# Two heads decoded at a time, peer_v rows summed four at a time, and four moved steps in a hybrid decoder step

## The reference

```python
u, q, k, v, qi, ki, wi, g_conv, g_attn = project_inputs(x, pos, w_in)     # one big projection, rotary, GLU
conv_out = conformer_conv(u, prev, ...)                                    # 31 taps per channel, norm, silu, projection
attn_out = attention over the keys that the indexer's top-k selects        # prompt: 128 of up to 512; sample: 256 of 1028
m = sigmoid(g_conv) * conv_out + sigmoid(g_attn) * attn_out
h = layer_norm(ALPHA * x + m @ w_out, ln1)

def peer_ffn(h):
    q1, q2 = halves of h @ peer_w_query                                    # 8 heads, 2 x 64
    t1, i1 = top_k(q1 @ peer_keys1, 16)                                    # of 128 keys
    t2, i2 = top_k(q2 @ peer_keys2, 16)
    ts, j = top_k(t1[:, None] + t2[None, :], 16)                           # of 256 candidates
    eidx = (i1 * 128 + i2) at j                                            # 16 experts of 16384 a head
    g = softmax(ts)
    a = gelu(h . peer_u[eidx])                                             # 128 rows of 1024 a token
    return sum over (g * a) * peer_v[eidx]                                 # 128 rows of 1024 a token

y = layer_norm(ALPHA * h + peer_ffn(h), ln2)
```

## Time and profile before

| what | us |
|---|---|
| median of 3 runs | 2096.13 |
| lowest, highest of them | 2087.34, 2105.51 |
| the profiled execution's own time | 2089.12 |
| its span, first to last instruction | 2087.3 |
| DVE busy | 1282.2 (61%) |
| PE busy | 1449.6 (69%) |
| POOL busy | 1205.3 (58%) |
| moved by DMA | 682.74 MB, 327 GB/s in the mean |

### The profile page before, as it was taken

How to read it: one execution, slowest core, us unless ns; L and a number is a source line. 1 busy time by engine, 2 the same in 40 slices (tenths; PEclk the granted TensorE clock), 3 DMA queues, 4 the chain that set the end, 5 groups by cost and what they waited for, 6 DMA issues and landing times.

```text
span 2087.3 us, 19495 instructions
## 1 busy us (share of the span) xinstructions
PE 1449.6 (69%) x6117; PEld 578.3 (28%) x6117; DVE 1282.2 (61%) x3076; ACT 381.6 (18%) x1031; POOL 1205.3 (58%) x1107
## 2 busy tenths in 40 slices
PE   7899999778975657676658777855354356766435
PEld 3554444333320214342112332411111012221101
DVE  4429964881178499848949767577399974112341
ACT  1510011372000352110027221100010002100000
POOL 1003454485566658756766777677576665336664
PEclk9999999988997885688789878997575568889869
DMA  8728999799989978989999899999999979979997
GB/s 305 315 87 304 327 357 367 261 307 324 324 312 341 378 243 296 363 295 329 352 404 336 312 344 372 329 364 373 307 362 349 370 261 392 382 249 358 378 364 293
DMA packets 207458, 682.74 MB, mean 327 GB/s; under 512 B 26901, under 2 KB 54933, under 8 KB 200787
## 3 DMA queue, kind: packets, MB, share of 16 engines
q0 software_dynamic: 157376, 581.67, 76.4%
q1 hardware_dynamic: 42971, 90.66, 12.2%
q10 hardware_dynamic: 7008, 9.17, 1.2%
HBM read 668.88 MB, written 12.94 MB: 327 GB/s over the span
## 4 chain that ended last, share of the span: by engine, by line
PE 33%; DVE 19%; POOL 15%; issue 13%; DMA 8%; SPq 7%; ACT 2%; another core or an unknown queue 2%; POOLq 0%; ACTq 0%; DVEq 0%
POOL rings L906 15%; PE acc L1820 8%; DVE rings L2232 7%; PE acc L1380 7%; DMA rings<-peer_v,late 6%; PE wide L1380 3%; PE bank L1524 3%; DVE small L1884 3%; SPq L707 3%; PE wide L1404 2%; PE acc L1347 2%; SPq L715 2%; DVE uah L1887 1%; DVE soft_score L1887 1%
## 5 line engine op out<-in xcount | busy, mean ns | idle before, releaser
L906 POOL DMA_INDIRECT rings<-peer_u,late x544 | 611.8, 1125 | 428.6 <-DVE late L2232 166.7
L1820 PE MATMUL acc<-rings,z_stages 128*32 128x512 f32 x2048 | 554.5, 704 | 397.6 <-issue 211.4
L906 POOL DMA_INDIRECT rings<-peer_v,late x544 | 585.0, 1075 | 341.2 <-PE acc L1820 154.2
L2232 DVE CUSTOM_DVE_ANT_0 rings<-rings,uah 128x1024 f32<-128x1024 f32 x288 | 346.7, 1224 | 151.6 <-DMA rings<-peer_u,late 136.5
L2232 DVE CUSTOM_DVE_ANT_0 rings<-rings,late 128x1024 f32<-128x1024 f32 x256 | 308.6, 1223 | 99.3 <-DMA rings<-peer_u,late 94.6
L1820 PEld LDWEIGHTS acc<-rings,z_stages 128*32 128x32 f32 x2048 | 120.1, 120 | 771.0 <-issue 763.6
L1380 PE MATMUL acc<-rings 128*128 128x512 f32 (+1 forms) x352 | 147.3, 569 | 0.0
L1293 ACT COPY z_stages<-late 128x4 f32<-128x4 f32 x136 | 26.2, 198 | 523.0 <-PE acc L1820 329.9
L1553 PE MATMUL wide<-zt,ident_s 128*128 128x512 f32 x122 | 73.2, 700 | 20.9 <-issue 11.7
L1380 PEld LDWEIGHTS acc<-rings 128*128 128x128 f32 x352 | 62.5, 190 | 69.6 <-issue 68.9
L1667 PE MATMUL wide<-keep,soft_score 128*128 128x64 f32 x320 | 57.8, 335 | 33.3 <-ACT soft_score L1112 31.2
(11 more groups left out here) (298 smaller groups left out, 1594.4 us busy)
## 6 DMA issues: line engine op xcount, KB each, us to landing
rings<-w_in SPq DMA_DIRECT2D x36, 1024.0 KB, 7.5
rings<-peer_u,late POOLq DMA_INDIRECT x544
rings<-peer_v,late POOLq DMA_INDIRECT x544
z_rows<-z_stages ACTq DMA_DIRECT2D x30, 256.0 KB
soft_score<-ln SPq DMA_DIRECT2D x6, 1024.0 KB
zt<-z_rows SPq DMA_DIRECT2D x2, 2596.0 KB
w_out_s<-w_out POOLq DMA_DIRECT2D x1, 4096.0 KB, 17.0
w_query_s<-w_query POOLq DMA_DIRECT2D x1, 4096.0 KB, 14.0
```

What stands on the lines that cost most here:

```text
L906: nc.gpsimd.indirect_dma_start(ring[:, place, :], None, table, offs).then_inc(row_in[place], 16)
L1820: last = nc.tensor.matmul(acc_v[QUAD * j:QUAD * (j + 1), half * BLK:(half + 1) * BLK], lone[:, quad % LONE, j, QUAD - 1 - m:2 * QUAD - 1 - m],
L2232: V.tensor_tensor_reduce(out=ring[:, place, :], in0=ring[:, place, :], in1=h, scale=1.0, scalar=0.0, op0=ALU.mult, op1=ALU.add, accum_out= ...
```

## The change

- Routing: the decoding moves into a function, `decode`. Tiles two to four call it after every second head, for both heads at once, with operands twice as long, and raise `routed` by 2. Tile one and the sample keep one head at a time. The conversion of the key numbers (line 2016) moves into it.
- The sums: `expert_pair` becomes `expert_rows` with a count. The rows that are fetched by themselves in tiles one to three (80, 32 and 32) go four at a time; all others stay in pairs. A group is placed in PE's order at the due time of its last row.
- SP: `load_values(0, pages_of(0))` moves from behind `index_pages` in the fourth tile's front to `front_sample`, behind the loads of line 802 and ahead of the stores of the sample's outputs.
- The sample's first maximum on DVE is due 0.4 of a step later (9 planned us), its exponentials on ACT 0.2 of a step later.
- `CLOCK_S`: everything of the sample behind 0.84 is due 8 to 10 planned us later.

```diff
-    onehot = queries[:, 0:2 * PEER_TOPK * PEER_TOPK]
+    onehot = queries[:, 0:4 * PEER_TOPK * PEER_TOPK]
...
+    def rows_at_once(v, i):
+
+        return N_QUADS if v < LAST and i < EARLY_V[v] else N_QUADS // 2
...
-    CLOCK_S = ((0.0, 0.0), (0.04, 32.0), (0.21, 56.0), (0.48, 176.0), (0.84, 272.0), (1.18, 315.0), (1.3, 330.0))
+    CLOCK_S = ((0.0, 0.0), (0.04, 32.0), (0.21, 56.0), (0.48, 176.0), (0.84, 272.0), (0.845, 282.0), (1.18, 323.0),
+               (1.3, 338.0))
...
+    AT_S_FIRST = AT_S_ATT + 0.4 * S_ATT_STEP
...
                 for r in range(S_ROUNDS):
                     index_pages(r)
-                load_values(0, pages_of(0))
...
                                                     k=S_PER_ROUND)[:, :, k, :]).then_inc(sel_in, 16)
+            load_values(0, pages_of(0))
             sp.wait_ge(y_stored, 16 * (N_TILES - 2))
...
-                yield at + 0.2 * S_ATT_STEP
+                yield at + 0.2 * S_ATT_STEP if p else AT_S_FIRST
                 act.wait_ge(s_max, p + 1)
...
-        def expert_pair(v, i):
+        def expert_rows(v, i, count):
...
-            for k in (i, i + 1):
+            for k in range(i, i + count):
                 place, landed, _ = HOMES["v", v, k]
                 pe.wait_ge(row_in[place], landed)
             if i % N_QUADS == 0:
                 pe.wait_ge(diag_ready, quad + 1)
             for half in range(2):
-                for k in (i, i + 1):
+                for k in range(i, i + count):
...
-                    if number % 2:
-                        expert_pair(tile, number - 1)
+                    count = rows_at_once(tile, number)
+                    if number % count == count - 1:
+                        expert_rows(tile, number - count + 1, count)
...
+                decoded = 2 if 0 < t < S_T else 1
+                if hd % decoded == decoded - 1:
+                    yield tail_at(at + 0.7 * span, tokens_here)
+                    yield from decode(t, n, hd - decoded + 1, decoded, tail_at(at + 0.8 * span, tokens_here))
...
+        def decode(t, n, first, heads, later):
+
+            chain, e = chains[t], e_of[place_of(t)]
+            slots = slice(PEER_TOPK * first, PEER_TOPK * (first + heads))
+            found, rows = heads * PEER_TOPK, 2 * heads * PEER_TOPK
+            both = lambda x: x[0:n, 0:rows].rearrange("p (k s) -> p k s", s=2)
+            chain.mark(V.tensor_copy(top_if[0:n, first:first + heads], top_i[0:n, first:first + heads]))
+            chain.mark(V.tensor_scalar(both(c_rowu)[:, :, 0], c_idx[0:n, slots], 4, None, ALU.logical_shift_right))
+            chain.link(V.tensor_scalar(both(c_rowu)[:, :, 1], c_idx[0:n, slots], 15, None, ALU.bitwise_and))
+            chain.link(V.tensor_copy(c_row[0:n, 0:rows], c_rowu[0:n, 0:rows]))
+            ones = onehot[0:n, 0:rows * PEER_TOPK].rearrange("p (x j) -> p x j", j=PEER_TOPK)
+            chain.link(V.tensor_tensor(ones, c_row[0:n, 0:rows].unsqueeze(2).to_broadcast([n, rows, PEER_TOPK]),
+                                       iota16[0:n, :].unsqueeze(1).to_broadcast([n, rows, PEER_TOPK]), ALU.is_equal))
+            if heads > 1:
+                yield later
+            chosen = onehot[0:n, 0:rows * PEER_TOPK].rearrange("p (h k x) -> p h k x", h=heads, k=PEER_TOPK)
+            numbers = top_if[0:n, first:first + heads].rearrange("p h s j -> p h (s j)")
+            chain.link(V.tensor_tensor(chosen, chosen, numbers.unsqueeze(2).to_broadcast(
+                [n, heads, PEER_TOPK, 2 * PEER_TOPK]), ALU.mult))
+            chain.link(V.tensor_reduce(c_found[0:n, 0:rows], ones, AX.X, ALU.add))
+            if first == 0 and t:
+                dve.wait_ge(e_trans, t)
+            chain.link(V.scalar_tensor_tensor(eidx_f[0:n, slots], both(c_found)[:, :, 0], float(PEER_NKEYS),
+                                              both(c_found)[:, :, 1], ALU.mult, ALU.add))
+            V.tensor_copy(e[0:n, slots], eidx_f[0:n, slots]).then_inc(routed, heads)
...
-            yield AT_S_ATT
+            yield AT_S_FIRST
             maximum(0)
```

More of the change, by code:

```diff
@@ L202, in _build @@
     c_idx = small[:, 640:768].bitcast(U32)
-    c_row = actT[:, 768:800]
-    c_rowu = actT[:, 800:832].bitcast(U32)
-    c_found = actT[:, 832:864]
+    c_row = actT[:, 768:832]
+    c_rowu = actT[:, 832:896].bitcast(U32)
+    c_found = actT[:, 896:960]
     iota16 = small[:, 768:784]
@@ L1998, in routing @@
             dve.wait_ge(key_copied, 4 * t + 2)
-            e, gate = e_of[place_of(t)], g_of[place_of(t)]
+            gate = g_of[place_of(t)]
             heads, keys = (S_HEADS, sk_s) if t == S_T else (PEER_HEADS, sk)
@@ L2015, in routing @@
                 yield tail_at(at + 0.4 * span, tokens_here)
-                chain.mark(V.tensor_copy(top_if[0:n, hd], top_i[0:n, hd]))
                 chain.link(V.tensor_tensor(
```

20 lines of the change are left out of this document (removed).

## The result

| | us |
|---|---|
| before, median of 3 (lowest, highest) | 2096.13 (2087.34, 2105.51) |
| changed, median of 3 (lowest, highest) | 2069.73 (2054.29, 2078.47) |
| ratio, 95% interval | 0.985, 0.9807 to 0.9893 |
| the changed kernel's profiled execution, its span | 2069.73, 2067.8 |

The change makes the kernel faster by 26 us by the two medians, or by 31 us (22 to 40) by the ratio with its interval. I had forecast 60 against the medians (53.5 against the profiled execution), so the direction is right and the size about twice too large; the time lies above my range.

What follows compares the result with a forecast made beforehand. No single engine bounds the span, so the bound was read by stretches where fetches stand still. Terms 21 + 4 + 1.5 + 22 + 5 = 53.5 us off 2089.1 gave 2035.6, stated as 2036, range 2020 to 2052.

Steps and rivals of the forecast that it cites:

- First V behind the sample's loads: Sample's start: V pages moved behind the sample's loads end the waits of DVE, ACT and POOL; 22 us, bounds 15 and 27.
- the hole closes in part (about 2050): Rival at the sample's start: loads land later or V's register loads delay SP, 14 of 22 us lost; chance 0.12.
- Rows four at a time: Tile one to two: four rows summed in 1.94 us, 20.3 us off PE's chain, routing starting near 564.4.
- The DMA can follow: 51 rows at 1.28 are 65 us, for 68 us left: Tile one to two: fetches at a free stretch's 1.28 us a row keep up with the faster sums.
- The cycle of two groups: Fours with 11 places: one landing and one sum, 8.3 us for 8 rows, under 8 times 1.28.
- if it doesn't hold, half of the 20.3 is lost: Tile one to two: the loss if the cycle of two groups does not stay under the fetches' time.
- Decoding: Routing of tiles two to four: two heads in 4.9 us, 6 us saved a tile, first pair known after 17.4 us.
- the three changes of tiles: Steps into tiles two, three and four from fours and paired decoding: 21, 4 and 1.5 us, together 26.5.
- The later maximum and tail: Sample: first maximum due 9 us later, tail 8 to 10 planned us later; together 5 us.
- The maximum's term (-1): Sample's first maximum and exponentials due later: 1 us lost, bounds -6 and 4.
- The tail's (6, bounds 0 and 10): Sample's later tail: PE sums rows in its 11 us wait, POOL's 12.9 us wait shrinks by 6; 6 us gained.
- The chance of 0.92 for faster: Whole kernel: chance of being faster by more than about 1% (21 us); within 1% 0.05, slower 0.03.

Runs made afterwards that it cites:

- after_again: The whole change, unaltered, run again on a chip with fast SP, against the kernel before: 2017.34 us beside 2048.85, ratio 0.9839.
- only_v_move: The kernel before with only the first pair's V pages moved behind the sample's loads: 2051.25 us beside 2050.31, ratio 1.0003.
- first_pair_single: The changed kernel with the first two heads of tiles two to four decoded singly: 2059.05 us beside 2091.67 for the kernel before, ratio 0.9828.

## Why the prediction was wrong

*The step that failed is "First V behind the sample's loads ... I take 22, near DVE's 23.2 (bounds 15 and 27)".* The mechanism was right: SP's order makes DVE, ACT and POOL stand, and the moved pages end or shorten that. The size was wrong, twice over. First, I priced the hole by what the standing engine loses. Made on purpose, 22.1 us of standing cost 10 us: for most of the hole the DMA engines stayed busy (a share of 1.06), and what was lost are the bytes not moved at its end and in the 20 us behind it (263 GB/s against 392 over 25 us, 8.2 us' worth). The floor of 15 (really POOL's 14.2) was no floor either. Two windows of the kernel before would have told it, 1465 to 1489 with its share of 1.03 and 1478 to 1508 with its 245 GB/s, and I had not asked for them; I had read the share in a free stretch and used it only for a rival. Second, the hole is there only when SP is late: at 75 us for the index pages instead of 104, the same move measured 1.0003. In the first pair of profiles the move's net, read by fetch numbers, was 6 us (36.2 less 19.0, less 11 given back). The rival "the hole closes in part (about 2050)" named this direction, by 14 of the 22.

*Rows four at a time: right, with the rate of the fetches as its limit.* Sums of 1.92 to 1.94 us for four rows, 19.5 us off PE (20.3 forecast), start at 565.1 and 567.6 where the DMA engines moved 395 and 385 GB/s (564.4 forecast). In the first profile, at 359 GB/s, the start was at 572.9, and 8.5 of the 20.3 were lost. The sub-step that failed there is "The DMA can follow: 51 rows at 1.28 are 65 us, for 68 us left". The 1.28 came from the 410 GB/s of a free stretch; at the 359 GB/s of this one a row takes 1.46 us and 51 rows take 74.5. My own could have warned me: the stretch to be shortened showed 320 GB/s at a share of 0.89, which scales to 360 at a full share. That is no ceiling, since the faster chips reached 385 to 396 there with fours, but 51 rows at 360 fill 74 us. The four waits of POOL that the profile does not explain, 7.8 us, are about the whole difference to after_again. The cycle of two groups is not what failed, nor is half of the gain lost by it as I had feared. I had named this end ("if it doesn't hold, half of the 20.3 is lost") for another reason than the one that came. The Trainium skill (TensorE: Matmul & The Clock Gate, Part 3: Packing small matmuls) says that small matmuls whose outputs lie in different column groups run at the same time; the traces agree: 8 records of two column groups take 1.91 us and 16 of four take 1.92 to 1.94.

*Decoding: right in every duration, and small.* 4.9 us a pair and 17.75 us to the first pair. As forecast, the wait for it takes back part of the 6 us a tile. Together with the fours, 26.5 us were forecast for the three changes of tiles and the two runs alone give 22 (20 and 2).

*The later maximum and tail: forecast 5, measured 13 and 15.* The maximum's term (-1) stands. The tail's (6, bounds 0 and 10) was too small: I had halved POOL's 12.9 us and given nothing for PE's own 11.0. That this time went into sums is my reading; no run tests it. Here, unlike at the sample's start, DMA had room: a share of 0.92 and 345 GB/s in 1800 to 1850 of the kernel before.

*The sum.* With what the parts measure alone, 20 + 2 + 0 + 13 = 35, and the whole measured 33 us on a chip of that kind; with a hole on the chip, some 10 more were to be expected, and some 8 fewer from the slower landings. That would be 35, and the first comparison gave 26 by the medians, 31 (22 to 40) by the ratio. Its two traces also lose 14.4 us in the last 80 fetches, which none of these terms holds. The 7 us between the profiled execution and the median stood against me as well: I forecast a median of 2036 by subtracting from an execution that lay near the lowest of its three. The chance of 0.92 for faster was deserved; the range was not, since its upper end let at most one of the two doubtful terms fail, and both were read off one execution.

What stays open: why the kernel before takes 2050 us in two sets and 2092 to 2099 in the other two, why SP is slow there, what POOL's unnamed waits are, and why the last 80 fetches take longer. The share taken by the hole in the whole change on a chip of the slower kind was not measured by itself.

## What to carry to other kernels

A stretch in which engines stand is worth what the resource behind them leaves unused in it: look at the DMA share and at the bytes moved in the very window of the hole, and in the one behind it until the stream is full again, before you price it by the idle time of an engine. Take the rate of transfers from the stretch that you want to shorten, and not from the best one of the trace. Where places are few, work out the cycle from release to release (issues, landing, the piece that stands before the sum, the sum at the clock that PE will have there); bigger groups pay only while that cycle is shorter than the transfers themselves. In tiles one to three the fours gained 20 us, with 11 places for their rows; put also on tile four's rows, which have 8, they lost 32. A hole that hangs on the pace of a queue of instructions should be looked for in more than one execution before it is counted.

## What the runs showed of the hardware that I had not expected

SP's pace differs from chip to chip, by half and more, with the same program. The 64 index pages took 74 to 75 us in all the traces of two sets and 104 to 129 us in the other traces. Single instructions show it. Start and duration in us of some of SP's instructions, first from only_v_move (75 us), then from first_pair_single (121 us):

```
1334.77 0.04 FUSED_REGOPS
1334.85 0.03 MOVE
1334.91 0.47 DMA_DIRECT2D
1335.42 0.27 TENSOR_LOAD
1335.72 0.15 FUSED_REGOPS
```

```
1346.66 0.69 MOVE
1348.10 0.01 DMA_DIRECT2D
1348.12 0.01 FUSED_REGOPS
1348.85 0.75 MOVE
1349.60 0.00 DMA_DIRECT2D
```

In the second, moves between registers take 0.7 us, or 0.7 us pass between two instructions, in stretches beside others at the usual pace. The chips on which SP is slow differ in two more things. They move fewer bytes in a busy stretch: 362 to 369 GB/s at a share of 0.96 to 0.98 in 496 to 565 us for the changed kernel and its variants, against 386 to 396 at 0.99 to 1.00; in 700 to 720 us the kernels that keep pairs move 408 to 411 GB/s on all chips. And only there has POOL waits that end with nothing of this program (`remote`): 12 to 21 fetches of each of the six traces wait so for over 0.4 us, 13 to 38 us in all, and none in the other eight. Whether all this has one cause wasn't tried.
